# The loop over sixteen experts written out in full, in place of a hardware loop over pairs of them

## The chip, the cores and the metric

The kernel runs on one core of one Trainium2 chip. The metric is the device time of one execution in microseconds (us). The core has five engines with an instruction stream each: TensorE (PE, with its weight loads shown apart as PEld), VectorE (DVE), ScalarE (ACT), GpSimd (POOL) and SyncE (SP), which here issues transfers. The streams meet only through semaphores.

## What is computed

Two layers of a diffusion backbone over 1024 latent tokens and 256 context tokens, width 1024. Each layer ends in an expert-choice mixture of sixteen SwiGLU experts: an expert picks its tokens (128 latent ones, 32 context ones in the first layer), and adds back its weighted result.

```
a = jnp.einsum('becd,edf->becf', xe, w_gate)
u = jnp.einsum('becd,edf->becf', xe, w_up)
y = jnp.einsum('becf,efd->becd', jax.nn.silu(a) * u, w_down)
y = y * g[..., None].astype(y.dtype)
out = jnp.zeros((b * n, d), y.dtype).at[flat].add(y.reshape(-1, d))
```

N_EXPERTS is 16, D_MODEL 1024, EXPERT_FF 1408. Everything is float32. The change is in the experts of the first layer, where latent and context tokens are routed as separate sets and share the weights of an expert.

## The kernel before

The kernel is a row of stages, each closed by a barrier of all engines. `expert_mixed_stage` is the experts of the first layer, called "the mixed stage" here; `expert_rows_stage` is those of the second, "the rows stage".

In the mixed stage the weights of one expert come in twelve pieces, numbered p = 0 to 11 (places of gate, up and down pieces are in GATE_AT, UP_AT, DOWN_AT; place 2 holds the last down piece of the expert before). A piece is up to 128 x 3 x 1024 numbers and passes through a ring of four slots:

- SP loads it into `mixed_raw` (L1336) when the piece four places before has been split and has been read by the context products.
- ACT rounds it into `mixed_high` (L1477), DVE takes the rest into `mixed_low` (L1543).
- PE first multiplies the 32 context tokens by the raw weights (`context`, L1387 and L1392), then the 128 latent tokens in three products of high and low parts (`latent`, L1399 to L1401).
- Between pieces PE turns the hidden layer (L1440) and the tokens of the next expert (L1452). DVE makes the context tokens of the next expert in `copy_xc` (L1557) after piece 10, and PE's piece 0 of the next expert waits for it. ACT makes silu of the context gate in L1499 and PE's next up piece waits for that.

Each engine runs the same function `turn(e, b)` for e = 0 to 16, where b is the buffer of the expert's tokens. `turns` decides how: experts 0, 15 and the rest piece of 16 are written out; experts 1 to 14 are a hardware loop (`Fori`) of seven rounds with an odd and an even expert in each. There e is a register, so the values that semaphores are waited for are registers too, computed by small instructions in the stream (lines L1296, L1373, L1418 and others), and SP adds a register to a transfer's address. A round ends with the step of the counter and a compare-and-branch (L1301). PE, ACT, DVE and SP each have such a loop; POOL has none here (its gathers and scatters are written out). The rows stage has a loop of the same build at L1755, which the change leaves alone.

"Crossing" below is the stretch from the start of piece 11 of one expert to the start of piece 1 of the next. From an even to an odd expert it holds the branch back; from an odd to an even one it lies inside the round. The crossing from expert 0 to 1 enters the loop, that from 14 to 15 leaves it.

Of the kernel before, what the change touches and what calls it, by code (L numbers as in the profile page):

```python
# [40 lines left out]
NE = 16  # L41
# [1208 lines left out]
def expert_mixed_stage(nc, m, d, name, layer):  # L1250
# [4 lines left out]
    with stage_of(nc) as ctx:  # L1255
# [41 lines left out]

        def turns(engine, body):

            body(0, 0)  # L1300
            with engine.Fori(0, NE // 2 - 1) as i:  # L1301
                body(i * 2 + 1, 1)
                body(i * 2 + 2, 0)
            body(NE - 1, 1)
            body(NE, 0)

        def later(e):
            return not isinstance(e, int) or e > 0
# [12 lines left out]
        @block.sync  # L1321
        def _(sp):
            at = (layer * 6 + 5) * D
            sp.dma_start(r.gates, d["mrow"][0:1, at:at + D].to_broadcast((P, D))).then_inc(gates_in, 16)
            for g in range(4):
                row = d["mrow"][1:2, at + g * QD:at + (g + 1) * QD]
                sp.dma_start(r.gatesc[32 * g:32 * g + 32, :], row.to_broadcast((32, QD))).then_inc(gates_in, 16)

            def turn(e, b):
                for p in range(TURN):  # L1330
                    if exists(e, p):
                        owner, kind, u, nj = whose(e, p)
                        need(sp, low_done, before(e, p, SLOTS))
                        need(sp, ctx_done, before(e, p, SLOTS))
                        src = units[bass.ds(owner * FJ + GJ[u][0], nj), :, kind * D:(kind + 1) * D]
                        sp.dma_start(r.raw[:, p % SLOTS, 0:nj, :], src.rearrange("j p n -> p j n")).then_inc(  # L1336
                            piece_in[p % SLOTS], 16)
            turns(sp, turn)
# [28 lines left out]
        def _(pe):  # L1367
# [97 lines left out]
            for part in range(3):  # L1465
                turn_x(0, part)
            turns(pe, turn)

        @block.scalar
        def _(act):  # L1470
# [60 lines left out]
            for p in range(SLOTS):  # L1531
                split(0, p)
            turns(act, turn)

        @block.vector
# [901 lines left out]
```

## Time and profile before

| | |
|---|---|
| median of 3 runs | 3567.95 us (3567.95 to 3575.17) |
| the profiled execution | 3570.9 us, of which the span from first to last instruction is 3569.0 us |
| PE busy | 3032.9 us, 85% of the span |
| DVE, ACT, POOL busy | 2068.5, 1790.0, 479.2 us |
| mixed stage, from the first matmul of expert 0 | 885.6 to about 2040 us |
| bytes moved by DMA | 726.17 MB |

Times inside the profile are microseconds from the start of the span. "Idle before" an instruction is how long its engine sat still before it, and the name behind "<-" is what ended that; "issue" there means that nothing the profile shows ended it. PEclk is the granted TensorE clock as a share of 2.4 GHz, so 0.50 is 1.2 GHz.

### The profile page before, as it was taken

The numbers are of one execution on the slowest core, as the hardware profiler recorded it, in microseconds if no ns is written. First come the engines' busy times: TensorE is split into PE (matmuls) and PEld (weight loads), VectorE is DVE, ScalarE is ACT, GpSimd is POOL, SyncE is SP. The second block draws the span as 40 slices with busy tenths as digits, with TensorE's granted clock in tenths as the row PEclk, the third lists the DMA queues.
The fourth block names the chain that finished last, engine by engine and source line by source line (L and its number), as shares of the span: only waits on it lengthen the run. The fifth ranks groups of instructions, "written<-read, shape, count | busy, mean of one in ns | idle before, by whom it ended". The sixth has DMA issues, their size and how long they took to land. (4 is left out here: it accounts for less than half of the span.)

```text
span 3569.0 us, 61226 instructions
## 1 busy us (share of the span) xinstructions
PE 3032.9 (85%) x24750; PEld 2475.3 (69%) x24750; DVE 2068.5 (58%) x2213; ACT 1790.0 (50%) x2016; POOL 479.2 (13%) x250
## 2 busy tenths in 40 slices
PE   6599787976999999999999939992957999999993
PEld 2488643543787788877878737661436999999993
DVE  0522374344666666666666644554256888888884
ACT  2411153333555555555545445765235777777773
POOL 1111142002010101011010003332020000000000
PEclk8699899987999999999999959996978999999997
DMA  7211100237777777777777531101236999999995
GB/s 317 73 36 42 48 1 25 100 118 315 264 257 249 265 250 257 260 251 250 270 249 257 198 96 36 30 24 45 105 149 234 357 354 358 386 362 357 357 361 176
DMA packets 137950, 726.17 MB, mean 203 GB/s; under 512 B 10709, under 2 KB 13525, under 8 KB 109829
## 3 DMA queue, kind: packets, MB, share of 16 engines
q1 hardware_dynamic: 125064, 684.99, 51.0%
q0 software_dynamic: 12288, 37.75, 4.6%
q8 instruction: 176, 2.88, 0.3%
q14 instruction: 38, 0.30, 0.0%
q10 hardware_dynamic: 384, 0.24, 0.0%
HBM read 680.90 MB, written 42.04 MB: 203 GB/s over the span
## 5 line engine op out<-in xcount | busy, mean ns | idle before, releaser
L1543 DVE TENSOR_TENSOR mixed_low<-mixed_raw,mixed_high 128x3072 fp32r<-128x3072 f32 (+1 forms) x192 | 592.8, 3094 | 393.7 <-ACT mixed_high L1477 390.8
L1477 ACT CAST mixed_high<-mixed_raw 128x3072 fp32r<-128x3072 f32 (+1 forms) x192 | 489.3, 2552 | 492.1 <-DMA mixed_raw<-in_moe 479.0
L1964 DVE TENSOR_TENSOR rows_low<-rows_raw,rows_high 128x2816 fp32r<-128x2816 f32 x188 | 581.3, 3093 | 79.4 <-ACT rows_high L1908 70.2
L1908 ACT CAST rows_high<-rows_raw 128x2816 fp32r<-128x2816 f32 x188 | 479.4, 2559 | 115.1 <-PE ps L1815 66.6
L1399 PE MATMUL ps<-mixed_high,mixed_xhi 128*128 128x384 f32 (+1 forms) x1024 | 345.9, 338 | 0.5 <-DVE mixed_low L1543 0.5
L1813 PE MATMUL ps<-rows_high,rows_xhi 128*128 128x352 f32 x1024 | 337.5, 330 | 6.0 <-issue 4.5
L1400 PE MATMUL ps<-mixed_low,mixed_xhi 128*128 128x384 f32 (+1 forms) x1024 | 331.4, 324 | 0.0
L1401 PE MATMUL ps<-mixed_high,mixed_xlo 128*128 128x384 f32 (+1 forms) x1024 | 331.2, 323 | 0.0
L1815 PE MATMUL ps<-rows_high,rows_xlo 128*128 128x352 f32 x1024 | 329.9, 322 | 0.0
L1814 PE MATMUL ps<-rows_low,rows_xhi 128*128 128x352 f32 x1024 | 329.6, 322 | 0.0
L1387 PE MATMUL ps<-mixed_raw,mixed_xc 128*32 128x96 f32 (+1 forms) x8192 | 197.9, 248 | 69.6 <-issue 31.5
L1387 PEld LDWEIGHTS ps<-mixed_raw,mixed_xc 128*32 128x32 f32 x8192 | 167.3, 113 | 99.9 <-issue 68.0
L1399 PEld LDWEIGHTS ps<-mixed_high,mixed_xhi 128*128 128x128 f32 x1024 | 194.4, 190 | 18.3 <-issue 2.2
L1813 PE MATMUL ps<-rows_high,rows_hthi 128*128 128x256 f32 x704 | 201.4, 286 | 3.0 <-issue 3.0
L1814 PE MATMUL ps<-rows_low,rows_hthi 128*128 128x256 f32 x704 | 200.1, 284 | 0.0
L1815 PE MATMUL ps<-rows_high,rows_htlo 128*128 128x256 f32 x704 | 200.1, 284 | 0.0
L1813 PEld LDWEIGHTS ps<-rows_high,rows_xhi 128*128 128x128 f32 x1024 | 193.4, 189 | 6.6 <-issue 6.6
L1400 PEld LDWEIGHTS ps<-mixed_low,mixed_xhi 128*128 128x128 f32 x1024 | 194.9, 190 | 0.0
L1401 PEld LDWEIGHTS ps<-mixed_high,mixed_xlo 128*128 128x128 f32 x1024 | 194.4, 190 | 0.0
L1814 PEld LDWEIGHTS ps<-rows_low,rows_xhi 128*128 128x128 f32 x1024 | 194.2, 190 | 0.0
L1815 PEld LDWEIGHTS ps<-rows_high,rows_xlo 128*128 128x128 f32 x1024 | 193.0, 189 | 0.0
L497 PE MATMUL ps<-h_hi_r,w_hi_r 128*128 128x512 f32 (+1 forms) x432 | 158.1, 366 | 12.3 <-POOL w_lo_r L486 12.3
(286 smaller groups left out, 5861.2 us busy)
## 6 DMA issues: line engine op xcount, KB each, us to landing
rows_raw<-in_moe_rows SPq DMA_DIRECT2D x192, 1408.0 KB, 8.0
mixed_raw<-in_moe SPq DMA_DIRECT2D x144, 1536.0 KB, 6.4
ring_r<-in_ada_w SPq DMA_DIRECT2D x24, 2048.0 KB, 17.4
mixed_raw<-in_moe SPq DMA_DIRECT2D x48, 1024.0 KB, 6.7
w_raw_r<-in_ev_in SPq DMA_DIRECT2D x18, 512.0 KB, 3.5
w_raw_u<-in_od_in SPq DMA_DIRECT2D x16, 512.0 KB, 3.6
x_res<-ring_r SPq DMA_DIRECT2D x10, 512.0 KB, 2.6
x_norm<-ring_r SPq DMA_DIRECT2D x10, 512.0 KB, 2.9
```

Source lines behind the costliest of these rows:

```text
L497: pe.matmul(out, wh, xh, start=(k == 0), stop=False)
L1387: mm = pe.matmul(out, r.xc[:, b, k, :], w[:, :, k * P + 32 * g:k * P + 32 * g + 32], start=(k == 0), stop=(k == K - 1), tile_position=(0, ...
L1399: pe.matmul(out, x_high_part, w_high_part, start=first, stop=False)
L1400: pe.matmul(out, x_high_part, w_low_part, start=False, stop=False)
L1401: return pe.matmul(out, x_low_part, w_high_part, start=False, stop=last)
L1477: act.copy(r.high[:, p % SLOTS, 0:nj, :], r.raw[:, p % SLOTS, 0:nj, :]).then_inc(high_done, 1)
L1543: dve.tensor_tensor(r.low[:, p % SLOTS, 0:nj, :], r.raw[:, p % SLOTS, 0:nj, :], r.high[:, p % SLOTS, 0:nj, :].bitcast(F32), ALU.subtract). ...
L1813: pe.matmul(out, x_high_part, w_high_part, start=first, stop=False)
L1814: pe.matmul(out, x_high_part, w_low_part, start=False, stop=False)
L1815: return pe.matmul(out, x_low_part, w_high_part, start=False, stop=last)
L1908: act.copy(high[:, p % SLOTS, :], raw[:, p % SLOTS, :]).then_inc(high_done, 1)
L1964: dve.tensor_tensor(low[:, p % SLOTS, :], raw[:, p % SLOTS, :], high[:, p % SLOTS, :].bitcast(F32), ALU.subtract).then_inc(low_done, 1)
```

## The change

The hardware loop is replaced by a Python loop, which writes every turn into the program. `e` is then a number everywhere: the small register instructions, the loop's counter and its branch disappear, every wait is for a constant, and addresses of transfers are constants. For e = 0, 15 and 16 the code comes out as before. The order of work on each engine is the same.

```diff
@@ -1297,12 +1297,8 @@
 
         def turns(engine, body):
 
-            body(0, 0)
-            with engine.Fori(0, NE // 2 - 1) as i:
-                body(i * 2 + 1, 1)
-                body(i * 2 + 2, 0)
-            body(NE - 1, 1)
-            body(NE, 0)
+            for e in range(NE + 1):
+                body(e, e % 2)
 
         def later(e):
             return not isinstance(e, int) or e > 0
```

On TensorE this is the end of a round before: the last down products of an even expert, the turn of its hidden layer, the counter and the branch (the row behind the branch is the code of expert 15, reached after the last round).

```order
L1399 MATMUL ps<-mixed_high,mixed_hthi 128x512
L1400 MATMUL ps<-mixed_low,mixed_hthi 128x512
L1401 MATMUL ps<-mixed_high,mixed_htlo 128x512
L1440 MATMUL ps<-ident_sb,mixed_h 128x128 x2
L1301 REGISTER_ALU
L1301 COMPARE_AND_BRANCH
L1387 MATMUL ps<-mixed_raw,mixed_xc 32x96 x32
```

And this is TensorE at the same place now, between two experts (line numbers are four lower).

```order
L1395 MATMUL ps<-mixed_high,mixed_hthi 128x512
L1396 MATMUL ps<-mixed_low,mixed_hthi 128x512
L1397 MATMUL ps<-mixed_high,mixed_htlo 128x512
L1436 MATMUL ps<-ident_sb,mixed_h 128x128 x2
L1383 MATMUL ps<-mixed_raw,mixed_xc 32x96 x32
```

The counter and the branch are gone, and the next expert's context products stand right behind the transposes. TensorE's listing grows from 5167 to 8438 rows.

On SyncE the end of the round, with the transfers of three pieces and the instructions that compute waits and addresses, was this.

```order
L1336 DMA mixed_raw<-in_moe 128x2x1024
L1296 REGISTER_ALU
L1336 ISA
L1336 DMA mixed_raw<-in_moe 128x2x1024
L1296 REGISTER_ALU
L1336 ISA
L1336 DMA mixed_raw<-in_moe 128x3x1024
L1301 REGISTER_ALU
L1301 COMPARE_AND_BRANCH
```

Now the queue holds transfers alone, with their waits on constants.

```order
L1332 DMA mixed_raw<-in_moe 128x3x1024 x8
L1332 DMA mixed_raw<-in_moe 128x2x1024 x2
L1332 DMA mixed_raw<-in_moe 128x3x1024 x3
L1332 DMA mixed_raw<-in_moe 128x2x1024
L1332 DMA mixed_raw<-in_moe 128x3x1024 x6
```

No transfer has changed its place among the others. ACT's and DVE's listings grow from 963 to 1193 and from 1254 to 1606 rows in the same way.

## Rows read from the trace of the kernel before

**Rows 1.** The page: span, busy time of engines, and an instruction queue

```profile
span 3569.0 us, 61226 instructions
PE 3032.9 (85%) x24750; PEld 2475.3 (69%) x24750; DVE 2068.5 (58%) x2213; ACT 1790.0 (50%) x2016; POOL 479.2 (13%) x250
...
q14 instruction: 38, 0.30, 0.0%
```

**Rows 2.** Busy time in one round of the mixed stage

```profile
core 0: us, PE busy (x) PEld busy (x) DVE busy (x) ACT busy (x) POOL busy (x), PEclk, DMA share, GB/s
...
1250.44:1395.94 145.50, 136.64 (x1759) 117.09 (x1759) 93.98 (x84) 73.99 (x66) 17.09 (x8) 0.99 0.76 258
```

**Rows 3.** Waits of PE, 936 to 2040 us: total, times, longest

```profile
PE ps L1387 <- issue: 31.5, 22, 4.9
PE ps L1387 <- ACT mask_sb L1499: 26.1, 31, 3.1
PE ps L1387 <- DVE mixed_xc L1557: 7.9, 8, 1.4
```

**Rows 4.** PE's timeline where piece 0 of experts 3 and 4 begins

```profile
1103.81 2.79 PE L1387 MATMUL ps<-mixed_raw,mixed_xc 128*32 128x96 f32 x64 [4.07 <-issue]
...
1176.39 1.53 PE L1387 MATMUL ps<-mixed_raw,mixed_xc 128*32 128x96 f32 x64 [1.39 <-DVE mixed_xc L1557]
```

**Rows 5.** The six crossings with the branch back, columns as in Rows 2

```profile
1093.71:1111.05 17.34, 13.27 (x134) 10.97 (x133) 11.78 (x15) 5.43 (x5) 0.00 (x0) 0.90 0.56 198
...
1825.08:1844.05 18.97, 14.20 (x133) 11.60 (x132) 11.68 (x15) 7.95 (x5) 0.00 (x0) 0.82 0.56 199
sum 109.17, PE 82.57 PEld 68.47 DVE 70.57 ACT 35.63 POOL 0.00; mean PE 13.76 PEld 11.41 DVE 11.76 ACT 5.94 POOL 0.00
```

**Rows 6.** PE's idle stretch before expert 3, and the stretch behind it

```profile
1099.75:1103.81 4.06, 0.00 (x0) 0.01 (x1) 2.42 (x2) 0.32 (x2) 0.00 (x0) 0.95 0.37 147
1103.81:1106.60 2.79, 2.79 (x65) 2.51 (x65) 0.04 (x1) 2.79 (x2) 0.00 (x0) 0.50 0.03 6
```

**Rows 7.** Instruction queue in one round, 1030.05 to 1176.39: packets, MB, share

```profile
q8 instruction: 16, 0.26, 0.7%
```

**Rows 8.** Instruction queue in the rows stage's loop, 2790 to 3450

```profile
q8 instruction: 3, 0.05, 0.0%
```

**Rows 9.** PE's timeline in the rows stage, one row per expert

```profile
2882.13 0.54 PE L1858 MATMUL ps<-ident_sb,rows_h 128*128 128x128 f32 x3 [1.64 <-DVE rows_h L1976]
2932.44 0.55 PE L1858 MATMUL ps<-ident_sb,rows_h 128*128 128x128 f32 x3 [1.57 <-DVE rows_h L1976]
2982.74 0.54 PE L1858 MATMUL ps<-ident_sb,rows_h 128*128 128x128 f32 x3 [1.64 <-DVE rows_h L1976]
```

**Rows 10.** The seven crossings inside a round

```profile
1022.61:1035.89 13.28, 11.89 (x134) 9.64 (x133) 9.44 (x14) 6.54 (x5) 0.00 (x0) 1.00 0.74 255
...
sum 93.39, PE 83.71 PEld 67.50 DVE 63.46 ACT 44.27 POOL 0.00; mean PE 11.96 PEld 9.64 DVE 9.07 ACT 6.32 POOL 0.00
```

**Rows 11.** The crossings into the loop and out of it

```profile
950.67:962.89 12.22, 11.88 (x134) 9.71 (x133) 8.99 (x14) 5.48 (x5) 0.00 (x0) 1.00 0.80 281
1971.49:1984.52 13.03, 11.89 (x134) 9.74 (x133) 10.23 (x14) 6.32 (x5) 0.00 (x0) 1.00 0.68 238
```

**Rows 12.** Piece 3 of experts 1, 3, 5, 7, 9, 11, 13: first and sum

```profile
973.00:982.41 9.41, 6.35 (x93) 5.93 (x93) 5.83 (x7) 5.08 (x5) 1.63 (x1) 1.00 0.78 286
...
sum 50.37, PE 44.55 PEld 41.63 DVE 38.81 ACT 30.05 POOL 2.74; mean PE 6.36 PEld 5.95 DVE 5.54 ACT 4.29 POOL 0.39
```

**Rows 13.** ACT's loop instructions: duration in ns, least, median, most

```profile
L1301 ACTq FUSED_REGOPS  x7: 59/59/70, 959.2 to 1835.6; - x7
L1301 ACTq ALU_OP  x7: 35/35/35, 1103.8 to 1979.5; - x7
L1301 ACTq COMPARE_BRANCH  x7: 40/45/50, 1103.8 to 1979.5; - x7
```

**Rows 14.** Waits that are instructions of their own, same columns

```profile
L1296 DVEq EVENT_SEMAPHORE  x259: 21/21/2707, 893.3 to 2045.6; - x130
L1296 ACTq EVENT_SEMAPHORE  x215: 17/17/17, 893.3 to 2039.2; - x108
```

## The prediction

> **What bounds the kernel now.** I begin with the page [rows 1]: one execution has a span of 3569.0 us, and TensorE is busy for 3032.9 us of it, more than any other engine. That is a mean over stages, so I look at one round of the loop that is changed [rows 2]: of 145.50 us PE is busy for 136.64, DVE for 93.98, ACT for 73.99. PE sets the pace there, and only what shortens PE's idle time of some 9 us a round can shorten the stage. The list of waits says what that idle time is [rows 3]: 31.5 us "issue" (22 times, up to 4.9 us), 26.1 us for ACT's silu of the context gate, 7.9 us for DVE's context tokens. The first is nearly half.
>
> The timeline says where the "issue" is [rows 4]. Before piece 0 of expert 3 PE sits for 4.07 us and nothing releases it; before piece 0 of expert 4, where no branch lies, it sits for 1.39 us and DVE releases it. I went along PE's timeline from piece to piece and found the first kind at each even-to-odd crossing and nowhere else: six idle stretches of 3.4 to 4.9 us, before experts 3, 5, 7, 9, 11 and 13, about 25 us in all. The loop has seven rounds, so six branches back. So the reader is to see a stall that belongs to the branch, on the engine that bounds the stage.
>
> Why it stalls is in the queue that carries instructions: in one round it moves 16 packets, 0.26 MB [rows 7], for 1759 matmuls and 1759 weight loads [rows 2]. PE's code of a round is fetched anew each time. The loop of the rows stage moves 3 such packets in 660 us [rows 8], so its code stays on the chip, and there the timeline goes in even steps of 50.3 us with the same short wait on DVE [rows 9], with the branch and without it. A branch back to code that is no longer held costs 4 us; to code that is held, nothing that can be seen.
>
> **What the change removes.** First the loop's own instructions: ACT's take 59 + 35 + 45 ns a round [rows 13], seven rounds about 1.0 us. PE's wait registers cost it nothing: in its timeline a gate piece takes 5.85 us in expert 0, where the waits are constants, and 5.84 us inside the loop.
>
> Second the stall, with all that follows it. PE does nothing for 4.06 us and then runs at a granted clock of 0.50, the 1.2 GHz level, for the next 2.79 us [rows 6]; the 64 small matmuls take 2.79 us there and 1.53 us where PE had sat for 1.39 us only [rows 4]. I therefore don't count the stall alone but whole crossings, from the start of piece 11 to the start of piece 1, where PE has the same work. The six with a branch back take 109.17 us together, 17.34 the first and 18.97 the last [rows 5].
>
> A rule of the Trainium skill speaks against this change: the page "Advanced Engine Details and Errata", section "Control Flow Timing", gives a compare-and-branch about 108 ns. By it the sum would be 7 x 0.108 = 0.8 us, an estimate, and nothing could be measured. The page "Runtime: NRT & Kernel Launch", section "Instruction fetch mechanics", says on the other hand that a taken branch whose target is not in the window of held pages waits for a fetch; by that rule the stall goes, and this case's trace agrees with the second page, with 4.06 us.
>
> **What takes its place.** The bound of a crossing without the branch is what PE waits for instead. Inside a round the seven odd-to-even crossings take 93.39 us, 13.34 each; they hold the wait for DVE's context tokens [rows 10]. The one into the loop takes 12.22 and the one out of it 13.03 [rows 11]; both go, like the six, to an odd expert. The mean over these nine is (93.39 + 12.22 + 13.03) / 9 = 13.18 us. I take it rather than the 12.22, since PE comes sooner and the transfer, ACT and DVE behind it have less of a lead:
>
> 109.17 - 6 x 13.18 = 109.17 - 79.08 = 30.1 us.
>
> With 13.34 it would be 29.1, with 12.22 it would be 35.9. The 1.0 us of loop instructions is inside these crossings on PE; on ACT, DVE and SP it lies beside PE's work and I give it nothing. If that cover is gone it is worth 1 us at most.
>
> **What it adds.** No work, no transfer, no wait on another event. Code: PE fetches 16 packets a round already, so its traffic stays. But ACT, DVE and SP, whose rounds are short, now read fresh code. A round holds 66 ACT and 84 DVE instructions [rows 2] and 24 transfers; waits are instructions too, 215 and 259 over sixteen experts [rows 14], 59 a round. That is 233 instructions, six rounds more of them are 1400. A PE round is 0.26 MB for 3518 instructions, 74 bytes each; 1400 are 104 KB. If these engines use the other instruction queue, whose packets are 0.30 MB / 38 = 7.9 KB [rows 1], that is 13 fetches more. I cost them at nothing, because code in a straight line can be asked for ahead: PE passes some fourteen page ends a round with no idle that repeats there. If none of them were hidden, each could cost what PE's branch costs, 4.06 us. So the bounds are 0 and 13 x 4.06 = 53 us, and I take 0, as PE's rows are the nearest.
>
> **Where the lead could be missing.** The stall also gave the other engines 4 us to get ahead. The one odd expert that no stall precedes is expert 1, and its piece 3 takes 9.41 us, of which 3.06 is a wait for ACT that itself waited for a weight transfer. The other six take (50.37 - 9.41) / 6 = 6.83 us [rows 12]. That is 2.58 us more. Even experts, which no stall precedes either, take 6.3 to 7.0 us in the same piece, so I read expert 1 as the loop's filling and not as the price of a missing stall; it stays as it is.
>
> **Rivals.**
> 1. Forecast: the crossings cost 13.2 us. 3570.9 - 30.1 = 3540.8 us. Chance 0.60.
> 2. More comes back: the six go like the entry (35.9) and the wait in expert 1 goes too (2.58): 38.5 us, 3532.4. For it: entry and six both lead to an odd expert. Against: piece 3's wait is before any branch. Chance 0.15.
> 3. The lead is given back: each odd expert pays expert 1's 2.58 us once the stall is gone: 6 x 2.58 = 15.5, gain 14.6 us, 3556.3. For it: the waits of 0.3 to 1.1 us for ACT in each expert show that this chain is close. Against: the even experts. Chance 0.13.
> 4. It doesn't do what it says: the idle is not the branch's but of something at that place that the profile doesn't show, and only about 1 us goes: 3569.9. Against it: the rows stage, and that leaving the loop after expert 14 costs no 4 us. Chance 0.05.
> 5. Slower: ACT's and DVE's code fetches are not hidden. 13 x 4.06 = 53 us against 30.1: 3593.6. It decides from 30.1 / 4.06 = 7.4 unhidden fetches on. For it: silu on ACT is what PE waits for in every expert, with no slack. Against: PE streams without a loss. Chance 0.07.
>
> **How the numbers follow.** The profiled execution is 2.95 us above the median of the runs, 3567.95, and inside their range; against the median the forecast would be 3537.9. I give 3539, between the two. A measurement of this kernel tells about 0.2%, 7 us, from no change. Rivals 1 to 3 are faster by more than that: 0.88. Rival 4 is within it: 0.05. Rival 5 is slower: 0.07. The range leaves out rivals 4 and 5, 0.12, and a little of each end: from 3528 (rival 2 against the median, less a microsecond or two) to 3557 (rival 3).
>
> **What would show it.** In the changed kernel each even-to-odd crossing should take 12 to 13.5 us at a granted clock of 1.00; PE's "issue" waits in the stage should fall from 31.5 to under 8 us; the waits for ACT and DVE should grow by no more than some 6 us; a pair of experts should take 141 to 142 us throughout; the packets of PE's instructions should stay about 8 an expert; the second queue should grow by about 13 packets; gate pieces should stay at 5.84 us, and the rows stage at 50.3 us an expert. I am wrong if idle stretches of PE labelled "issue" stay at these crossings (rival 4), if piece 3 of odd experts takes over 9 us (rival 3), or if ACT or DVE show idle stretches of microseconds that no transfer and no engine ends (rival 5). The rows stage's loop now lies elsewhere in memory; should it no longer be held whole, its six branches back would show there too.

## The result, and the profile after

The changed kernel takes 3533.11 us (median of 4 runs, 3527.5 to 3539.82) against 3567.95 us; the ratio is 0.9898, 95% interval 0.9874 to 0.9923. Two more comparisons, in the experiments below, give 0.9913 and 0.9910. So 30 to 36 us go, 0.9 to 1.0%. The profiled execution lies at the low end of its kernel's times: its span is 42.0 us shorter than that of before [rows 1]. Two more profiles of the same kernel, taken in the later comparisons, have spans of 3530.0 and 3533.0 us; they are used below where one profile could mislead.

The page of the changed kernel: span, busy times, and the two instruction queues (packets, MB, share).

```profile
span 3527.0 us, 59842 instructions
PE 3017.9 (86%) x24750; PEld 2464.0 (70%) x24750; DVE 2070.8 (59%) x2213; ACT 1789.4 (51%) x2016; POOL 514.9 (15%) x250
...
q8 instruction: 163, 2.67, 0.3%
q14 instruction: 51, 0.42, 0.0%
```

PE's matmuls are as many, its busy time is 15 us less, which fits with fewer of them at a low clock. The second queue has grown from 38 packets to 51.

The list of PE's waits in the mixed stage (total, times, longest), which answers to [rows 3].

```profile
PE ps L1383 <- ACT mask_sb L1495: 28.2, 38, 1.6
PE ps L1383 <- issue: 10.1, 22, 1.1
PE ps L1436 <- DVE mixed_h L1573: 2.3, 4, 0.8
```

"Issue" has fallen from 31.5 to 10.1 us and its longest piece from 4.9 to 1.1. The wait for DVE's context tokens, 7.9 us before, is not in the list any more. The wait for ACT stays.

The six crossings from an even to an odd expert, columns as in [rows 5]: first, last, sum.

```profile
1087.06:1099.63 12.57, 11.95 (x133) 9.76 (x133) 8.60 (x14) 5.44 (x6) 0.00 (x0) 1.00 0.87 288
...
1788.85:1801.16 12.31, 11.93 (x133) 9.74 (x133) 8.61 (x14) 5.42 (x6) 0.00 (x0) 1.00 0.85 304
sum 76.70, PE 71.58 PEld 58.48 DVE 51.98 ACT 34.09 POOL 0.94; mean PE 11.93 PEld 9.75 DVE 8.66 ACT 5.68 POOL 0.16
```

The seven from an odd to an even expert, sum; piece 3 of expert 1; one pair of experts.

```profile
sum 89.82, PE 83.37 PEld 68.18 DVE 61.91 ACT 39.49 POOL 0.82; mean PE 11.91 PEld 9.74 DVE 8.85 ACT 5.64 POOL 0.12
...
970.89:977.55 6.66, 6.33 (x94) 5.94 (x93) 5.66 (x7) 4.13 (x5) 0.25 (x1) 1.00 0.95 343
...
1023.90:1163.10 139.20, 134.66 (x1758) 115.39 (x1759) 94.27 (x85) 76.39 (x67) 20.64 (x8) 1.00 0.80 271
```

Here is the account of this one execution, from these rows against those of before. The six crossings give 109.17 - 76.70 = 32.5 us. The other seven give 93.39 - 89.82 = 3.6 us [rows 10]. Piece 3 of expert 1 gives 9.41 - 6.66 = 2.75 us [rows 12]. From the first matmul of expert 0 to that of expert 15 the timeline shows 41.1 us less, so some 2 us more lie in small things, and the stages around it give and take about a microsecond. The granted clock is 1.00 in all crossings, where it had been 0.82 to 0.91 in the six [rows 5].

The other two profiles of the changed kernel say how much of this is the change. The sums of the six crossings, then of the seven:

```profile
sum 79.04, PE 71.51 PEld 58.47 DVE 53.21 ACT 36.73 POOL 1.66; mean PE 11.92 PEld 9.75 DVE 8.87 ACT 6.12 POOL 0.28
sum 78.79, PE 71.44 PEld 58.43 DVE 52.22 ACT 36.35 POOL 0.96; mean PE 11.91 PEld 9.74 DVE 8.70 ACT 6.06 POOL 0.16
sum 92.75, PE 83.28 PEld 68.13 DVE 62.31 ACT 43.30 POOL 0.82; mean PE 11.90 PEld 9.73 DVE 8.90 ACT 6.19 POOL 0.12
sum 94.01, PE 83.27 PEld 68.12 DVE 61.62 ACT 43.35 POOL 0.83; mean PE 11.90 PEld 9.73 DVE 8.80 ACT 6.19 POOL 0.12
```

So the six crossings give 30 to 32.5 us in every profile, and the 3.6 us of the seven belong to the first execution: in the others these crossings take as long as before, 93.39, to within 0.7 us. From expert 0 to 15 the two others are 38.8 and 34.1 us shorter than before.

One view of the kernel before, which the prediction did not use for PE, shows the branch itself: the instructions of the sequencer (the part of an engine that reads its stream, waits and branches) at the loop's line. PE's compare-and-branch in the mixed stage and in the rows stage (least, median, most, in ns; the least is the last one, which is not taken):

```profile
L1301 PEldq COMPARE_BRANCH  x7: 83/5140/5772, 1098.3 to 1977.0; - x7
...
L1755 PEldq COMPARE_BRANCH  x7: 76/208/231, 2840.2 to 3445.1; - x7
```

The branch takes 5.14 us in the mixed stage (3.37 to 5.77 where it is taken) and 0.21 us in the rows stage. On ACT it takes 0.045 us [rows 13]. That the long ones wait for code is seen in the trace's DMA packets. Inside each of the six long branches exactly one packet of the instruction queue starts, of 16 KB, and it lands 1.42 or 1.43 us before the branch ends. Inside the rows stage's branches there is none. The first long branch runs from 1098.29 to 1103.43; its packet is in the window 1101.00 to 1101.10:

```profile
q8 instruction: 1, 0.02, 60.9%
```

### The profile page after: what moved, and what is told of

Its sections match the earlier page's. It is cut to its first block and busy times, and to the rows that moved or that the text cites. A ratio compares the mean times of both kernels' runs of the same rounds, so it can differ in the third digit from the quotient of the medians.

```text
span 3527.0 us, 59842 instructions
## 1 busy us (share of the span) xinstructions
PE 3017.9 (86%) x24750; PEld 2464.0 (70%) x24750; DVE 2070.8 (59%) x2213; ACT 1789.4 (51%) x2016; POOL 514.9 (15%) x250
## 5 line engine op out<-in xcount | busy, mean ns | idle before, releaser
L1383 PE MATMUL ps<-mixed_raw,mixed_xc 128*32 128x96 f32 (+1 forms) x8192 | 188.0, 243 | 42.4 <-ACT mask_sb L1495 28.2
```

The lines of the kernel that those rows point to most:

```text
L1383: mm = pe.matmul(out, r.xc[:, b, k, :], w[:, :, k * P + 32 * g:k * P + 32 * g + 32], start=(k == 0), stop=(k == K - 1), tile_position=(0, ...
```

## The experiments

All expectations speak of the six even-to-odd crossings as "crossings". Each kernel was timed in five rounds against the kernel before on the same chip.

### TensorE alone, and the others alone

```diff
         def turns(engine, body):
 
+            if engine is nc.tensor:
+                for e in range(NE + 1):
+                    body(e, e % 2)
+                return
             body(0, 0)
```

> Only TensorE's stream is written out; ACT, DVE and SP keep their loops. Theory A (the gain is TensorE's six branches back to code that is no longer held): the six even-to-odd crossings fall from 109 to about 77 us and the kernel takes 3534 to 3541 us, nearly all of the gain. Theory B (the gain comes from register waits and branches on all engines, SP's addresses among them): TensorE alone gives less than half, over 3551 us.

> ACT, DVE and SP are written out, TensorE keeps its loop. Theory A: the six stalls of about 4 us stay, crossings 106 to 110 us together, the kernel within 5 us of before (3563 to 3573 us). Theory B: more than half of the gain is here, under 3551 us. If fresh code on ACT or DVE costs anything, it shows here as slower than before.

In the second kernel the condition is `engine is not nc.tensor`. TensorE alone: 3540.62 us, ratio 0.9924 (0.9911 to 0.9936), the six crossings 76.2 us together. The others alone: 3566.79 us, 0.9988 (0.9974 to 1.0001), the crossings 106.1 us. PE's waits in the kernel with TensorE alone written out, and then in the other:

```profile
PE ps L1391 <- ACT mask_sb L1503: 41.8, 36, 3.1
PE ps L1391 <- issue: 8.8, 26, 0.9
```

```profile
PE ps L1391 <- issue: 29.4, 15, 4.4
PE ps L1391 <- ACT mask_sb L1503: 25.5, 29, 3.0
PE ps L1391 <- DVE mixed_xc L1561: 8.9, 9, 1.4
```

The long "issue" waits go with TensorE's branches and stay with them. Theory A holds, theory B falls. The wait for ACT is 41.8 us in the first kernel: five times it is 2.3 to 3.1 us long, before piece 4, each time after a late weight transfer. I could not tell from one comparison whether this is TensorE alone or chance, so it was repeated beside the changed kernel.

> TensorE alone written out, beside the changed kernel on the same chip: tells whether the other engines' streams give anything beyond TensorE's. Theory A with nothing from the others: within 3 us of the changed kernel. If the shorter wait code of ACT, DVE and SP lets silu and weight transfers come sooner, it is 4 to 9 us behind it.

> The changed kernel once more, on the same chip as the other two, for its time and its spread: 3530 to 3540 us. If the spread of its runs comes from single waits of 2 to 3 us for silu before piece 4 of an expert (late weight transfers), a slower profiled execution than the first one's 3527.0 us has some of them, and a fast one has none.

TensorE alone: 0.9912 (0.9898 to 0.9926). The changed kernel: 0.9913 (0.9899 to 0.9928). They are the same within the intervals, which are some 5 us to each side. So constant waits and addresses on ACT, DVE and SP bring nothing that can be measured here. The changed kernel's second profile has waits of 2.64 and 2.13 us before piece 4 in two experts and a span of 3530.0 us; the third has waits of 2.64 and 3.00 and 3533.0 us; the first had one of 1.62 and 3527.0 us. That fits the idea that these waits make the spread of the runs, but three profiles don't show it.

### Two branches back in place of six

```diff
             body(0, 0)
-            with engine.Fori(0, NE // 2 - 1) as i:
-                body(i * 2 + 1, 1)
-                body(i * 2 + 2, 0)
-            body(NE - 1, 1)
-            body(NE, 0)
+            with engine.Fori(0, 3) as i:
+                for j in range(1, 5):
+                    body(i * 4 + j, j % 2)
+            for e in range(NE - 3, NE + 1):
+                body(e, e % 2)
```

> The loop has three rounds of four experts (1 to 12) on every engine, experts 13 and 14 are written out: two branches back in place of six. Theory A: two stalls are left, before experts 5 and 9, and four of six shares of the gain are there: 4 x 5.4 = 22 us, plus what fewer instructions of the loop give, so 3542 to 3549 us. Theory B (cost of register waits, which twelve experts still have): little gain, over 3555 us.

3549.38 us, 0.9943 (0.9930 to 0.9956): 18.8 us less than before, just under the expected 19 to 26. Two thirds of the whole gain of 31 us would be 20.7. The timeline has two stalls of over 4 us, before experts 5 and 9. The first, and the branch's row:

```profile
1243.00 2.73 PE L1387 MATMUL ps<-mixed_raw,mixed_xc 128*32 128x96 f32 x64 [4.46 <-issue]
```

```profile
L1301 PEldq COMPARE_BRANCH  x3: 83/5106/5447, 1237.1 to 1815.5; - x3
```

The gain goes with the number of branches taken, at about 5 us each, though the registers stay for twelve experts.

### The branch behind large matmuls

The order of work stays; TensorE's round begins one piece later.

```diff
-            turns(pe, turn)
+            turn(0, 0)
+            turn(1, 1, range(1))
+            with pe.Fori(0, NE // 2 - 1) as i:
+                turn(i * 2 + 1, 1, range(1, TURN))
+                turn(i * 2 + 2, 0)
+                turn(i * 2 + 3, 1, range(1))
+            turn(NE - 1, 1, range(1, TURN))
+            turn(NE, 0)
```

> TensorE's loop keeps seven rounds and six branches back, but a round now begins with piece 1 of the odd expert, so that the branch stands behind 24 large matmuls (4.2 us) in place of two small transposes behind a wait. Theory A with a fetch of about 5.6 us that starts when the sequencer reaches the branch: most of it is covered, 1 to 2 us of stall remain and the clock does not fall; gain 15 to 28 us, 3540 to 3553 us. Rival C (the engine must be empty before a branch is taken, or the fetch starts only then): the stalls are as long as before, at the new place, and the time is that of before within 5 us or worse.

3578.26 us, 1.0032 (1.0020 to 1.0044): 10 us slower than before. That is far from theory A's 3540 to 3553 us; rival C had "within 5 us or worse". The branch, PE's timeline around the first one, and the clock of the stretches behind it:

```profile
L1469 PEldq COMPARE_BRANCH  x7: 83/6385/7465, 1099.3 to 1988.2; - x7
```

```profile
1102.14 0.34 PE L1401 MATMUL ps<-mixed_high,mixed_xlo 128*128 128x384 f32 x1
1106.15 1.64 PE L1387 MATMUL ps<-mixed_raw,mixed_xc 128*32 128x96 f32 x33 [3.67 <-issue]
1108.85 1.50 PE L1387 MATMUL ps<-mixed_raw,mixed_xc 128*32 128x96 f32 x31 [1.06 <-issue]
```

```profile
1102.48:1106.15 3.67, 0.00 (x0) 0.00 (x1) 3.19 (x2) 0.49 (x1) 0.00 (x0) 1.00 0.45 180
1106.15:1108.85 2.70, 1.64 (x33) 1.29 (x34) 0.00 (x0) 2.67 (x1) 0.00 (x0) 0.51 0.02 6
1108.85:1112.69 3.84, 3.84 (x38) 3.56 (x39) 3.59 (x3) 0.08 (x1) 0.00 (x0) 0.50 0.27 41
```

The branch begins at 1099.3, while PE has matmuls to do until 1102.48. At first sight these 3.2 us are covered. But the branch takes 6.4 us here and not 5.1, and the DMA packets say why. Here is each kernel with long branches (the ends of matmuls are modelled, so the third and fourth columns are good to some tenths):

| kernel | long branches | branch begins before PE falls idle by, us | its packet starts after PE fell idle by, us | packet landed to branch's end, us | branch, us |
|---|---|---|---|---|---|
| before | 6 | 0.35 to 1.46 | 0.69 to 2.13 | 1.42 to 1.43 | 3.37 to 5.77 |
| the others alone | 6 | 0.34 to 1.49 | 1.27 to 1.68 | 1.36 to 1.42 | 4.15 to 5.31 |
| two branches back | 2 | 1.14 to 1.42 | 1.50 to 1.64 | 1.44 to 1.50 | 5.11 to 5.45 |
| the branch moved | 6 | 3.16 | 0.64 to 1.92 | 1.43 to 1.44 | 6.20 to 7.47 |
| rows stage too long, its mixed stage | 6 | 0.35 to 0.82 | 1.30 to 1.59 | 1.48 to 1.51 | 4.04 to 4.67 |
| rows stage too long, its rows stage | 2 | 2.90 to 2.91 | 0.59 to 0.90 | 1.40 to 1.41 | 5.98 to 6.24 |

In none of the 28 does the packet start before PE has run out of matmuls, however early the sequencer stands at the branch. So the branch gets longer by nearly all the work that lies ahead of it: the stall before it is 3.68 us in the mean here and 4.21 in the kernel before, half a microsecond shorter for 1.7 to 2.8 us more of cover. So rival C stands, best in its second half, "the fetch starts only then": none of the 28 speaks against it. Why the fetch waits, the profile does not say. The DMA share over the branch does not order them: of the six here the longest, 7.47 us, has the lowest, 0.63.

What makes the kernel slower than before comes behind the branch. A second wait of 1.05 to 1.60 us follows, 33 matmuls later in the first case, in all six; it ends 1.3 to 1.4 us after the next instruction packet has landed, as the branch did behind its own, so it is most likely the next page of code. And the low clock, 0.50, now lasts 6.8 to 10.2 us where it was 3.4 to 6.8, and meets large matmuls. From the start of piece 11 to the start of piece 2, over the six places, before and here:

```profile
sum 144.21, PE 117.61 PEld 101.15 DVE 80.13 ACT 55.19 POOL 0.00; mean PE 19.60 PEld 16.86 DVE 13.36 ACT 9.20 POOL 0.00
sum 157.54, PE 123.81 PEld 105.17 DVE 93.35 ACT 53.58 POOL 0.00; mean PE 20.64 PEld 17.53 DVE 15.56 ACT 8.93 POOL 0.00
```

Of the 13.3 us more, 6.2 are PE's busy time, by the clock, and the rest is idle; elsewhere in the stage this execution is shorter by 6 us.

### The other loop made too long

The same edit as for two branches, at L1755 in the rows stage, whose branch takes 0.21 us; the mixed stage is as before.

> The mixed stage is as before; the rows stage's loop, whose TensorE branches take 0.21 us, has four experts a round in place of two (three rounds, experts 13 and 14 written out), so that a round's TensorE code is about twice as long as the one that is held. Theory A (only a branch to code that is no longer held is dear): the two branches back now take about 5 to 7 us each, with new packets on TensorE's instruction queue; part is covered by the matmuls ahead, so the kernel is 3 to 16 us slower than before, though it takes four branches fewer. Theory D (the mixed stage's branches are dear for another reason, such as its waits or its small matmuls): the branches stay at 0.2 us and the time is that of before within 3 us.

3578.35 us, 1.0058 (1.0043 to 1.0072), 18 us slower than before though four branches fewer are taken. The branch, and PE behind the first one:

```profile
L1755 PEldq COMPARE_BRANCH  x3: 82/5978/6244, 2932.3 to 3350.6; - x3
```

```profile
2939.12 0.40 PE L1813 MATMUL ps<-rows_high,rows_xhi 128*128 128x352 f32 x1 [3.93 <-DVE rows_h L1976]
```

This is the strongest proof of theory A: the same loop, branches of 0.21 us, becomes one with branches of 5.98 and 6.24 us when its round no longer stays on the chip. PE's instruction queue moves 213 packets in place of 176. The two stalls, of 3.93 and 3.73 us, are 7.7 of the 18 us; theory A had 3 to 16. (The profile gives them to DVE, whose `rows_h` had come long before; it was the branch.) The steps from one expert to the next are 56.1 and 55.8 us where a branch lies and 50.5 to 51.5 in most others, against 50.3 before, so the rest is partly behind the stalls and partly spread over all experts. The spread part was not expected and led to the next runs.

### The rows stage written out

> Both expert stages are written out. Theory A: the rows stage's branches cost 0.2 us each and are hidden, so this takes the time of the changed kernel within 4 us, 3530 to 3542 us. If every branch cost something on the path, it would be more than 10 us faster than the changed kernel.

3540.06 us, 0.9943 (0.9929 to 0.9957), against 0.9913 for the changed kernel on the same chip: 10 us slower. The prediction had argued that straight code costs nothing; there it does. Which engine's code?

> As the changed kernel, and in the rows stage TensorE's stream alone is written out; the other engines keep their loop there. Theory E (each packet of TensorE's instructions goes over the same DMA engines as the weights and holds one of them up for about 1 us, which a stage with its DMA engines 93% busy can't hide): the stage's 33 more packets come with it, and it loses the same 8 to 14 us as with all engines written out. Theory F (the loss comes from ACT's, DVE's or SP's code): less than 3 us behind the changed kernel.

> As the changed kernel, and in the rows stage ACT, DVE and SP are written out while TensorE keeps its loop. Theory E: no further packets of TensorE's instructions, and the time of the changed kernel within 3 us. Theory F: 8 to 14 us behind it.

> The changed kernel beside the two, on the same chip: 0.991 of before.

> As the changed kernel, and in the rows stage SP's queue alone is written out, so that its transfers have constant waits and addresses; no other engine's code there is fresh. If the loss of 12 to 16 us that ACT, DVE and SP together brought comes from the transfers and how they are issued, it is here: 8 to 16 us behind the changed kernel (0.994 to 0.9955 of before). If it comes from fresh code of ACT or DVE, this takes the time of the changed kernel within 4 us (0.990 to 0.992 of before).

| written out in the rows stage | ratio to before | interval | rows stage in the profile, first to last matmul, us |
|---|---|---|---|
| nothing (the changed kernel) | 0.9910 | 0.9892 to 0.9927 | 826.1 |
| TensorE | 0.9912 | 0.9893 to 0.9931 | 831.7 |
| ACT, DVE and SP | 0.9945 | 0.9928 to 0.9963 | 836.2 |
| SP (another comparison) | 0.9913 | 0.9895 to 0.9931 | 825.1 |
| all four (the comparison above) | 0.9943 | 0.9929 to 0.9957 | 839.3 |

Theory E falls as the account of the loss: with TensorE's 33 more packets the median is that of the changed kernel (3532.14 and 3532.11 us). That these packets cost nothing at all is not shown. In the one profile the rows stage is 5.6 us longer with them, and the mixed stage happened to be shorter; the interval is 7 us to each side. Theory F holds: the loss of 0.35%, 12 us (16 between the medians), comes with ACT's, DVE's and SP's code, and SP's alone is not it. It is spread over the experts, at 51.3 us each in the mean in place of 50.5. From 2750 to 3440 us the second queue moves 10 packets, and 2 in the kernel with SP alone:

```profile
q14 instruction: 10, 0.08, 0.0%
```

Twelve microseconds for 8 packets is 1.5 us each, if it is the fetches at all. There is another difference. GpSimd's scatters, whose code is the same in all these kernels, with ACT, DVE and SP written out, and then with SP alone:

```profile
L1791 POOL DMA_INDIRECT x_res<-rows_ys,idx x16: 1550/4432/4458, 2740.4 to 3499.9; - x16
```

```profile
L1791 POOL DMA_INDIRECT x_res<-rows_ys,idx x16: 1550/1586/4529, 2728.9 to 3477.3; - x16
```

The scatter takes 4.43 us and not 1.59. In both kernels it is issued while DVE makes the same subtraction; what differs is by how little it comes behind it. With ACT, DVE and SP written out, and then in the changed kernel:

```profile
2895.65 3.09 DVE L1964 TENSOR_TENSOR rows_low<-rows_raw,rows_high 128x2816 fp32r<-128x2816 f32 x1 [0.21 <-DVE rows_ys L1995]
2895.77 4.44 POOL L1791 DMA_INDIRECT x_res<-rows_ys,idx  x1 [43.63 <-DVEq L1998]
```

```profile
2883.23 3.16 DVE L1960 TENSOR_TENSOR rows_low<-rows_raw,rows_high 128x2816 fp32r<-128x2816 f32 x1 [0.30 <-DVE rows_ys L1991]
2883.27 1.59 POOL L1787 DMA_INDIRECT x_res<-rows_ys,idx  x1 [46.25 <-DVEq L1994]
```

Over all fourteen profiles of this document, 210 of these scatters are issued beside the subtraction. The 160 that come 0.03 or 0.04 us behind its start take 1.6 us. The 50 that come 0.05 to 0.12 us behind it take over 4 us, and end 1.44 to 1.49 us after the subtraction does. So it looks as if a scatter that comes some hundredths of a microsecond later is held until the subtraction is over; no run moves it on purpose.

Whether the late scatter costs the stage its 12 us is not shown. Both kernels that lose have 15 long scatters of 16, and no other has more than 3. But in the mixed stage, too, the scatter goes from 1.61 to 4.72 us (medians) when ACT, DVE and SP are written out, and there nothing is lost (0.9913 against 0.9912). No wait of another engine in the rows stage is put down to the scatter. ACT and DVE were not tried one by one, so it stays open which of them costs the 12 us and by what.

## Why the prediction was right or wrong

**The mechanism.** "The stall belongs to the branch, on the engine that bounds the stage": right, and shown from three sides. TensorE alone gives the whole gain (0.9912 against 0.9913; 0.9924 in its first comparison), two branches in place of six leave two stalls and give some two thirds of it, and a loop with cheap branches gets dear ones when its round is made too long. The packet of code inside each long branch shows what is waited for. Rival 4, that the idle is not the branch's, is out.

**The size of a crossing.** I took 13.18 us for what stays. In the first profile it is 76.70 / 6 = 12.78, which would make the term 2.4 us too small; in the two others it is 13.17 and 13.13, and the six crossings give 30.1 and 30.4 us. So the term was right, and the first profile is a fast execution. Between the medians the gain is 34.8 us, 4.7 more than forecast, with an interval of some 9 us to each side of it; in the later comparisons it is 30.4 and 33.6. That the first of these meets the forecast so closely is partly luck, since single executions differ by 10 us and more.

**The odd-to-even crossings.** I left them alone. Their sum, 93.39 before, is 89.82, 92.75 and 94.01 in the three profiles, so a gain there is not shown. What did change is the wait in them. DVE's context tokens are in the list of waits in all five kernels whose TensorE loops, with 6.7 to 9.3 us, and in none of the nine profiles with TensorE written out. In five of the seven odd experts the weight transfer started in piece 9 had taken 7.4 us or more, where six of the seven even ones had 6.3 to 6.5; in the changed kernel's three profiles none takes over 6.9. Why that pattern stood, and why it went, is open.

**Expert 1.** I read its 2.58 us as the filling of the loop, "it stays as it is". It went, to 6.66 us, as rival 2 said. But waits of this size turn up in other experts in other executions (three to five of them in some kernels, with TensorE's loop and without), so it was neither filling nor the price of one missing stall: as far as the profiles show, it is a late transfer that comes by chance. This single event was a poor witness for rivals 2 and 3 alike.

**Rival 3.** The price of 2.58 us in each odd expert did not come: the wait for ACT is 28.2 us in all where it was 26.1, and piece 3 stays below 7.5 us in every odd expert. In the third profile of the changed kernel, though, the wait for ACT is 34.0 us and piece 3 takes 9.01 and 9.33 us in experts 3 and 5, over the 9 us that I had named as a sign of this rival. Two experts of seven, in one profile of three, are not its 15.5 us; a small price of the missing lead, a few microseconds, can't be told from chance here.

**Rival 5, fresh code.** The count of 13 fetches more on the second queue came out exactly: 38 to 51. Costing them at nothing was right in the mixed stage: with those 13 and TensorE's loop kept, the ratio is 0.9988. The reason that I gave, that straight code can be asked for ahead, is not enough, though: in the rows stage, with PE over 95% busy and the DMA engines at 93%, writing out ACT, DVE and SP loses 12 us. In the changed kernel's mixed stage PE is as busy, 96%, but the DMA share is 0.78. That may be what makes the difference; no run separates it.

**What would show it.** "Issue" below 8 us was not met: 10.1, and 13.8 and 13.4 in the two other profiles. Crossings of 12 to 13.5 us: four of the six, the other two took 13.78 and 13.69. Pairs of experts at 141 to 142 us were 138.9 to 141.2. PE's packets in the stage are 7 an expert, 112 against 124, where I said about 8. The 12 that are gone are two for each branch back, and with two branches back there are 116; that a branch makes two pages be fetched twice fits this count.

**The rule and the row.** The Trainium skill's 108 ns for a compare-and-branch ("Advanced Engine Details and Errata", section "Control Flow Timing") lies between the branches to code that is held, 0.21 us on PE and 0.045 us on ACT; it says nothing of the 5.14 us. The rule of the Trainium skill's page "Runtime: NRT & Kernel Launch", section "Instruction fetch mechanics", that a taken branch out of the held pages waits for a fetch, decides here. The trace agrees with it: one packet of code lands inside every long branch and none inside a short one. The window of two pages that the section speaks of does not fit TensorE here: a round of the rows stage is 33 / 6 = 5.5 packets of 16 KB and is held.

## What to carry to other kernels

Look up how long the compare-and-branch itself takes on each engine before judging a hardware loop: on TensorE it was 0.2 us where a round's code stayed on the chip and 3.4 to 7.5 us, plus a slow clock behind it, where it did not. Moving the branch behind other work did not hide it here. Write out the stream of the engine whose branch is dear and leave the others: TensorE alone gave all there was, and writing out ACT, DVE and SP as well cost 12 us in the rows stage, by a cause that is not found. Making a loop's round longer to save branches can turn every cheap branch into a dear one.

## What the runs showed of the hardware

- A branch back on TensorE: 5.14 us (median, with the last one that is not taken) in the mixed stage, 6.39 with the branch at another place, 5.98 and 6.24 in the rows stage with four experts a round, 0.21 with two. With two experts a round the rows stage's TensorE code stays on the chip (3 instruction packets in 660 us [rows 8]); the mixed stage's, 3518 matmuls and weight loads a round [rows 2], does not.
- In all 28 long branches one 16 KB packet of code starts inside the branch, 0.59 to 2.13 us after PE fell idle and never before, and the branch ends 1.36 to 1.51 us after it has landed. Work that was handed over ahead of the branch makes the branch longer and the stall hardly shorter: 3.16 us of work left 3.68 us of stall, 0.35 to 1.46 us left 4.21.
- A second, shorter wait of 1.05 to 1.60 us can follow behind the branch, after 33 matmuls in the case shown.
- The same GpSimd scatter took 1.59 us when it was issued 0.03 us behind the start of DVE's subtraction, and 4.43 us when it was issued 0.12 us behind it.
